# Weights of the head quads rounded and subtracted 1024 columns at a time

## The reference

```
h = rmsnorm(x);  proj = h @ w_in
y = [ mLSTM (4 heads) | retention (4 heads) | gated DeltaNet (8 heads) ](proj)   # each with its state, gate and head norm
x = x + rmsnorm(y @ w_out)
h = rmsnorm(x);  x = x + rmsnorm( square(relu(h @ w_up)) @ w_down )             # D_MODEL 2048, D_FF 8192
```

## Time and profile before

| | |
|---|---|
| median of 3 runs | 3106.57 us (3105.53 to 3106.79) |
| the profiled execution | 3103.61 us, its span 3102.1 us |
| mean granted TensorE clock | 0.995 |
| busy share: TensorE, VectorE, ScalarE, GpSimd | 98%, 62%, 50%, 3% |
| matmul records, VectorE, ScalarE records | 22980, 3992, 3588 |
| weight loads (RAW) | 256 KB each, median 3.7 us from issue to landing |

### The profile page before, as it was taken

One profiled execution on the slowest core, in us unless ns is written; L12 is line 12 of the kernel. 1 busy time (PEld: TensorE's weight loads), 2 busy tenths in 40 slices (PEclk: granted clock), 3 DMA queues, 4 the chain that ended last, 5 costly groups with the idle time before them and its releaser, 6 DMA issues.

```text
span 3102.1 us, 66910 instructions
## 1 busy us (share of the span) xinstructions
PE 3046.1 (98%) x22980; PEld 2977.7 (96%) x22980; DVE 1922.9 (62%) x3992; ACT 1548.7 (50%) x3588; POOL 85.2 (3%) x162
## 2 busy tenths in 40 slices
PE   8999999999999999999999999999999999999998
PEld 7999999998999999999989999999989999999997
DVE  7688886656545545455586888856565454554555
ACT  6577775545434334334455677755453343343343
POOL 1100000000000000000001000000000000000000
PEclk9999999999999999999999999999999999999999
DMA  6544445453444444444445444454444444444444
GB/s 215 190 152 148 142 148 172 154 181 134 165 163 163 166 162 164 170 163 164 153 150 183 144 148 148 148 171 158 162 135 165 161 165 169 160 168 162 163 163 157
DMA packets 267223, 499.89 MB, mean 161 GB/s; under 512 B 34640, under 2 KB 39904, under 8 KB 267040
## 3 DMA queue, kind: packets, MB, share of 16 engines
q1 hardware_dynamic: 244080, 443.58, 43.4%
q0 software_dynamic: 14752, 51.05, 4.6%
q10 hardware_dynamic: 8208, 2.81, 0.4%
HBM read 475.32 MB, written 22.01 MB: 160 GB/s over the span
## 4 chain that ended last, share of the span: by engine, by line
PE 87%; DVE 7%; ACT 2%; issue 2%; DMA 2%; SPq 0%; POOL 0%; ACTq 0%; DVEq 0%; POOLq 0%
PE PU L521 77%; PE PABCD L521 3%; PE PF L521 3%; PE PE_ L521 3%; DVE WL L1338 2%; ACT AE L913 1%; DMA RAW<-in_w 1%; DVE Y L1360 1%; PE PABCD L524 1%; DVE X L1367 1%; ACT WH L913 1%; ACT Y L913 0%; DMA out_sout<-Y 0%; DVE HL L1343 0%; DVE AE L1719 0%
## 5 line engine op out<-in xcount | busy, mean ns | idle before, releaser
L521 PE MATMUL PU<-HH,WH 128*128 128x288 f32 x4000 | 1233.0, 309 | 21.1 <-DVE HL L1343 10.2
L913 ACT ACTIVATE WH<-RAW 128x512 fp32r<-128x512 f32 x1669 | 966.0, 621 | 564.6 <-PE PU L521 461.0
L1338 DVE TENSOR_TENSOR WL<-RAW,WH 128x512 fp32r<-128x512 f32 x1668 | 1075.1, 687 | 264.8 <-ACT WH L913 251.0
L521 PE MATMUL PU<-HH,WL 128*128 128x288 f32 x4000 | 1178.2, 295 | 0.0
L521 PE MATMUL PU<-HL,WH 128*128 128x288 f32 x4000 | 1171.0, 296 | 0.0
L521 PEld LDWEIGHTS PU<-HH,WH 128*128 128x128 f32 x4000 | 753.7, 188 | 47.7 <-issue 29.6
L521 PE MATMUL PU<-UH,WH 128*128 128x288 f32 x2560 | 759.1, 297 | 2.8 <-DVE UL L1504 1.9
L521 PEld LDWEIGHTS PU<-HL,WH 128*128 128x128 f32 x4000 | 750.1, 189 | 9.3 <-issue 3.3
L521 PE MATMUL PU<-UL,WH 128*128 128x288 f32 x2560 | 755.2, 295 | 0.0
L521 PEld LDWEIGHTS PU<-HH,WL 128*128 128x128 f32 x4000 | 755.2, 189 | 0.0
L521 PE MATMUL PU<-UH,WL 128*128 128x288 f32 x2560 | 752.6, 294 | 0.0
(11 more groups left out here) (274 smaller groups left out, 2257.9 us busy)
## 6 DMA issues: line engine op xcount, KB each, us to landing
RAW<-in_w SPq DMA_DIRECT2D x1669, 256.0 KB, 3.7
SIN<-in_sin POOLq DMA_DIRECT2D x32, 512.0 KB, 4.9
out_sout<-Y POOLq DMA_DIRECT2D x32, 512.0 KB, 5.2
BC<-gate_rows POOLq DMA_DIRECT2D x32, 304.0 KB, 4.6
AUX<-in_aux POOLq DMA_DIRECT2D x32, 152.0 KB, 3.9
X<-in_x SPq DMA_DIRECT2D x4, 576.0 KB, 7.1
out_y<-X SPq DMA_DIRECT2D x8, 288.0 KB, 2.1
out_sout<-SOUT ACTq DMA_DIRECT2D x32, 64.0 KB, 2.3
```

Source lines behind the costliest of these rows:

```text
L521: return nc.tensor.matmul(out, lhsT, rhs, start=start, stop=stop, skip_group_check=True)
L913: return nc.scalar.activation(out, in_, f, **kw)
L1338: tt(WL[s % 2][:, k], RAW[c][:], WH[s % 2][:, k].bitcast(F32), ALU.subtract).then_inc(sem("lo_ready"), 1)
```

## The change

The four RAW buffers become one tile RAWS of 16 blocks, with RAW[i] as views of it, so that two neighbouring pieces lie side by side. In quads of the kinds gdn, ret and mls, pieces from 4 to 19 are worked on in pairs by `lo_pair`, and those from 6 to 19 by `hi_pair`, with the even piece's slot for both; the odd piece's slot is empty. Pieces 5 and 20 are rounded singly. A pair waits for both its loads or, on VectorE, for both pieces being rounded, and raises its semaphore by two. The kinds first, out, up and down stay as they are. The loads stay four for each unit.

```diff
--- before.py
+++ after.py
@@ -155,7 +155,8 @@
         Y = sb("Y", [128, NC_, T])
         HH, HL = sb("HH", [128, NC_, T], F32R), sb("HL", [128, NC_, T], F32R)
         UH, UL = sb("UH", [128, NC_, T], F32R), sb("UL", [128, NC_, T], F32R)
-        RAW = [sb(f"RAW{i}", [128, NC_ // 4, HD]) for i in range(4)]
+        RAWS = sb("RAWS", [128, NC_, HD])
+        RAW = [RAWS[:, 4 * i:4 * i + 4] for i in range(4)]
         WH = [sb(f"WH{i}", [128, NC_, HD], F32R) for i in range(2)]
         WL = [sb(f"WL{i}", [128, NC_, HD], F32R) for i in range(2)]
         con = {n: sb(n, list(d[n].shape)) for n in d if n.startswith("c_")}
@@ -349,6 +350,12 @@
             steps = gate_steps[engine]
             return sem(f"gate_steps_{engine}"), l * len(steps) + len(steps) - steps[::-1].index(name)
 
+        def pieces_at(p, kind):
+
+            if kind not in ("gdn", "ret", "mls") or p == 20:
+                return 1
+            return 0 if p % 2 else 2
+
         def aux_count(kind, x):
 
             n, nk, hk, par, pair = x
@@ -368,7 +375,7 @@
 
                 k = slice(4 * c, 4 * c + 4)
                 src = d["w"][unit, :, k] if isinstance(unit, int) else d["w"][bass.ds(unit, 1), :, k].rearrange("a p k m -> p (a k) m")
-                sp.dma_start(RAW[c][:], src).then_inc(sem(f"raw_in{c}"), 16)
+                sp.dma_start(RAW[c], src).then_inc(sem(f"raw_in{c}"), 16)
 
             for c in range(4):
                 k = slice(4 * c, 4 * c + 4)
@@ -925,7 +932,17 @@
 
                     act.wait_ge(sem("unit_done"), 4 * Q + s + 1)
                 k = slice(4 * c, 4 * c + 4)
-                fn(WH[s % 2][:, k], RAW[c][:]).then_inc(sem("hi_ready"), 1)
+                fn(WH[s % 2][:, k], RAW[c]).then_inc(sem("hi_ready"), 1)
+
+            def hi_pair(Q, p):
+
+                s, c = divmod(p, 4)
+                if c == 0:
+                    act.wait_ge(sem("unit_done"), 4 * Q + s + 1)
+                for j in (c, c + 1):
+                    act.wait_ge(sem(f"raw_in{j}"), 16 * (4 * Q + s + 1))
+                k = slice(4 * c, 4 * c + 8)
+                fn(WH[s % 2][:, k], RAWS[:, k]).then_inc(sem("hi_ready"), 2)
 
             def prenorm(l, e, gain, Q):
 
@@ -1289,7 +1306,12 @@
                     if t % 2 and not (last_head and t == 13) and not (kind in ("first", "up_first") and t < 7):
                         if last_head and t == 15:
                             hi_part(Q, 11, joined)
-                        hi_part(Q, (t + 1) // 2 + 4, joined)
+                        piece = t // 2 + 5
+                        count = 1 if piece == 5 else pieces_at(piece, kind)
+                        if count == 2:
+                            hi_pair(Q, piece)
+                        elif count:
+                            hi_part(Q, piece, joined)
                     if last_head and t % 8 == 7:
 
                         for u in {7: (), 15: (7, 15), 23: (23,), 31: (31,)}[t]:
@@ -1335,7 +1357,16 @@
                     dve.wait_ge(sem("unit_done"), 4 * Q + s + 1)
                 dve.wait_ge(sem("hi_ready"), 16 * Q + p + 1)
                 k = slice(4 * c, 4 * c + 4)
-                tt(WL[s % 2][:, k], RAW[c][:], WH[s % 2][:, k].bitcast(F32), ALU.subtract).then_inc(sem("lo_ready"), 1)
+                tt(WL[s % 2][:, k], RAW[c], WH[s % 2][:, k].bitcast(F32), ALU.subtract).then_inc(sem("lo_ready"), 1)
+
+            def lo_pair(Q, p):
+
+                s, c = divmod(p, 4)
+                if c == 0:
+                    dve.wait_ge(sem("unit_done"), 4 * Q + s + 1)
+                dve.wait_ge(sem("hi_ready"), 16 * Q + p + 2)
+                k = slice(4 * c, 4 * c + 8)
+                tt(WL[s % 2][:, k], RAWS[:, k], WH[s % 2][:, k].bitcast(F32), ALU.subtract).then_inc(sem("lo_ready"), 2)
 
             def prenorm_lo(l, which, gain, chunks=range(NC_)):
                 for c in chunks:
@@ -1827,7 +1858,12 @@
                     if last_head and t == 15:
                         evac(Q, 0, kind, l, x)
                     if t % 2 and not (kind in ("first", "up_first") and t < 8):
-                        lo_part(Q, t // 2 + 4, l if last_head else None)
+                        piece = t // 2 + 4
+                        count = pieces_at(piece, kind)
+                        if count == 2:
+                            lo_pair(Q, piece)
+                        elif count:
+                            lo_part(Q, piece, l if last_head else None)
                     if kind == "first":
                         rotate(t, l * H_B, 0, FIRST_ROTATE_SLOTS)
                     if kind == "ret" and not front:
```

## The result

The changed kernel takes 3168.81 us (median of 4 runs, 3166.91 to 3171.97) against 3106.05 us, a ratio of 1.0206 (95% interval 1.0193 to 1.0219): 2.1% slower, 62.8 us by the medians. The direction and the place were forecast, the size was not: 48 us were expected. The median lies 1.2 us under the top of the range, which ended at 3170; the ratio's middle applied to the 3106.57 us of the forecast is 3170.6, just outside it. The profiled execution took 3171.97 us against 3103.61, so 68.4 us are to be found in the traces.

What follows compares the result with a forecast made beforehand. TensorE, busy 98% of the span, was taken to bound the kernel. Gdn quads 42, retention quads 5 and the fourth retention and mls quads 1 sum to 48 us: 3154 us, range 3135 to 3170.

Steps and rivals of the forecast that it cites:

- The wait at slot 1: Gdn quads: VectorE's first pair waits for piece 5's rounding, delaying the root chain and TensorE's slot 6 by 1.98 us.
- Slots 7, 9 and 11: Gdn quads, TensorE: 0.48 us lost at slot 7, 0.10 won by slot 9, 0.19 lost at slot 11.
- slots 13 and 17: Gdn quads: subtraction pairs in the same pattern with some more room, counted between 0 and 0.2 us.
- The clock: TensorE: new gaps of 2 us might lower the granted clock; nothing was charged for it.
- Retention quads: Slot 3 rounds pieces 6 and 7 together, delaying K's spread: half of six times 1.7, 5 us, bounds 0 and 10.
- The fourth retention quads and the mls quads: Same pairs, but K's spread precedes slot 3 or steps lie several us apart: 1 us, bounds 0 and 8.
- More waits: Rival: loads run together and later, so retention, mls and gdn quads lose more; 63 us, 3169; chance 0.12.
- Hidden anyway: Rival: TensorE's wait vanishes if slot 1's pair starts 1.98 us earlier, at 300.56 or before; 3106; chance 0.05.
- faster: Rival: same condition as hidden, and 4.3 us of TensorE idle time come back; 3102; chance 0.03.
- The first wait alone: Rival: only slot 1's wait costs, later pairs run in its shadow and loads come in time; 32 us, 3138; chance 0.18.
- The savings on VectorE and ScalarE: Fewer, longer records save 17 us of VectorE and some 17 of ScalarE, hidden by TensorE's work.

Runs made afterwards that it cites:

- the first pair alone: Kernel before, with only pieces 4 and 5 subtracted together in slot 1 of gdn, ret and mls quads, all roundings single: 3152.08 us.
- the gap filled: Changed kernel plus 12 matmuls ahead of TensorE's wait in slot 6 of each gdn quad, their result overwritten: 3159.05 us.
- Their own run: Kernel before, with pairs in the first three retention quads of each layer alone: 3117.48 us.
- piece 5 early: Changed kernel with all pairs, but ScalarE rounds piece 5 ahead of the eight activations of slot 1 in gdn quads: 3120.89 us.

## Why the prediction was right and wrong

**The wait at slot 1** was right in mechanism and nearly in size. Undoing it by moving one rounding took 62.8 us down to 16.3, and it alone made 47.5. In a quad whose clock stays up the interval between root squares is 42.37 to 42.65 us, on average 42.5, against 40.2 before, so 2.3 us; the prediction's sum was 2.55. The terms: from piece 5 to slot 6 4.06 us (3.98 predicted), but ScalarE reached piece 5 about 0.3 us earlier against TensorE than in the trace of before, so slot 6 is 1.7 us late and not 1.98. With the first pair alone, where all roundings are single, it is 2.05 late, so these 0.3 us go with the paired roundings; by what way was not followed. In the first gdn quad of each layer slot 6 is 2.92 us late, where 2.89 were forecast. The stall of all sixteen is 38 us, where 42 were counted: 53.8 us that TensorE falls back in them, less the clock's part below.

**Slots 7, 9 and 11.** Slot 7 comes 323.54 - 321.61 - 1.46 = 0.47 us late (0.48). Slot 9 wins 0.22 where 0.10 were counted: from 323.54 to 326.39 it is 2.85 instead of 3.07. Slot 11 loses 0.08 and not 0.19: from 326.39 to 329.28 it is 2.89 instead of 2.81. Behind it some 0.2 us more are lost up to the next slot 6, within what was allowed for slots 13 and 17.

**The clock** is the step that failed most: a term that was put at nothing measured 15.7 us. The prediction said of it that the new gaps might lower the granted clock, "for which I charge nothing", and gave no reason for the nothing. It fell at the gap of slot 6 in 8 of the 16 gdn quads, to 0.50 for about 3.4 us in four and 6.8 us in four. What a fall costs is read from the intervals between root squares, each against the same interval in the run with the gap filled, where the clock stayed up: 43.45 to 43.95 against 42.38 to 42.73 for a short fall, 1.1 to 1.2 us, and 44.8 to 45.1 against 42.37 for a long one, 2.4 to 2.8. In the fourteen intervals the changed kernel took 608.64 us, the one with the gap filled 595.98, and the one before 562.61 (183.38 to 464.22 and 1725.93 to 2007.70): 46.0 us of loss, 33.4 that stayed with the gap filled and 12.7 that went when TensorE had work in it. Over the whole of the sixteen quads it is 53.8 us against 39.6, and as 1.5 of the 39.6 are the one fall left in that run, the clock cost 15.7 and the stall 38.1. That the idle gap is what lowers the clock is shown by this run; why one gap does it and another of like length does not is open. Two gaps that differ by the fall behind them:

```profile
408.20 0.86 PE L528 MATMUL PABCD<-Y,PMS 128*128 128x128 f32 x6 [1.92 <-DVE Y L1665]
```

```profile
453.31 0.85 PE L528 MATMUL PABCD<-Y,PMS 128*128 128x128 f32 x6 [1.57 <-DVE Y L1665]
```

After 1.92 us of idle the clock fell in the first; after 1.57 it stayed in the second. But at 234.12 it fell for the long time after 1.58. The Trainium skill (TensorE: Matmul & The Clock Gate, the section on psum-queue depth-cycling) tells of a kernel in which TensorE's brief idles between groups of matmuls came so often that the clock swung between its two levels. The trace agrees that short idles do it, with eight falls at sixteen gaps; that they must be frequent it does not bear out, for here there is one in some 42 us.

**Retention quads.** The mechanism was right, the term was too small: 16.0 us instead of 6. In the third quad, ScalarE and TensorE as in the earlier trace rows:

```profile
118.93 1.06 ACT L920 ACTIVATE WH<-RAWS 128x1024 fp32r<-128x1024 f32 x1 [3.54 <-DMA RAWS<-in_w]
119.90 0.42 ACT L920 ACTIVATE LG<-GATE 128x288 f32<-128x288 f32 x1
120.23 0.29 ACT L920 ACTIVATE Y<-Y 128x128 f32<-128x128 f32 x1
```

```profile
120.78 0.52 PE L531 MATMUL PABCD<-c_ident,Y 128*128 128x128 f32 x3 [1.56 <-ACT Y L920]
```

The pair starts as soon as the load of piece 7 is there, the spread of K 1.30 after it (1.31 predicted), and TensorE, 0.26 later, had waited 1.56. The error was to count half of six such quads. Their own run gives 12.4 us, 2 us a quad. In its trace TensorE is 0.8 to 1.9 us later at K's spread in each of the six, 7.1 in all; the rest stands in smaller waits behind it (RHS, and the mask of L1615 twice 0.5) and in a fall of the clock, at 1604, that the trace of before has not. The fourth retention quads and the mls quads made 2.9 and 3.8 us, each near what the measurement can tell, where 1 was counted for both. Of the 2.9, 1.9 are TensorE's wait for L1769 (L1738 before) for that head's front, 1.45 us instead of 0.50 in both layers, a step that the prediction did not look at.

**Together** 38.1 us of stall in gdn quads (42 forecast), 15.7 for the clock there (0) and 14.6 for the retention and mls quads with the falls in them (6) are the 68.4 of the two profiled executions; by the medians it is 62.8. The clock's falls probably differ from execution to execution, which would fit the spread from 3166.91 to 3171.97, but one trace does not show it. The prediction's own list of rivals had no case for the clock. "More waits" came out at the measured time (3169) by luck: it was right that the retention quads cost more, but its 63 us hold 45 of stall in the gdn quads and nothing for the clock.

**The rivals.** "Hidden anyway" and "faster" named the right point from which they decide: with piece 5 early the wait is hidden. The 4.3 us of idle time did not come back even then, so faster was not to be had. "The first wait alone" was priced at 32 us; alone it made 47.5, the clock included. The savings on VectorE and ScalarE were forecast too small, 17 us each against 22.9 and 31.5, which changes nothing in the sum: as forecast, they gave TensorE nothing.

## What to carry to other kernels

Merging two records moves the first one's result and its buffer's release to the second one's time; before doing it, look up where the second one's input is made in the producer's order and what stands behind the merged record in the consumer's. When the busiest engine waits, price the gap's effect on its clock too: here it added two fifths to the stall. And time saved on engines that the bound engine does not wait for was worth nothing here: 14 us of VectorE and 15 of ScalarE in the gdn quads gave back none.

## What the runs showed of the hardware that was not expected

- Gaps of 1.6 to 3.0 us in a stream of matmuls that is otherwise dense for 40 us lowered the granted clock to 0.50 in 8 of 16 cases, for about 3.4 or 6.8 us; gaps of 1.9 to 3.3 us, with the first pair alone, in 9 of 16.
- Twelve useless matmuls in such a gap made the kernel about 11 us faster than without them.
- A rounding of 1024 columns on ScalarE takes 1.06 us and lets the next start after 0.97 (118.93 to 119.90); two of 512 take 2 x 0.52 = 1.04 start to start. A VectorE subtraction of 1024 takes 1.22 and lets the next start after 1.14, against 2 x 0.60. So a merge of two that follow each other at once saves 0.06 to 0.07 us on either engine. The busy time fell by more, 0.10 us for each of 240 pairs on VectorE and 0.15 for each of 210 on ScalarE; a likely reason, not followed, is that a record behind which the engine idles counts with its whole 0.69 or 0.62 us.
